# Two more weight splits on VectorE and the memory-weight scaling on ScalarE, in a two-layer decoder on one core

## What is computed

```python
z  = rmsnorm(h) @ w_in                        # columns for four token mixers
h += concat(gla(z_A), pool(z_B), topk_attention(z_C), gated_mlp(z_D)) @ w_out
q  = rmsnorm(h) @ xa_wq                       # cross-attention to 256 memory tokens
kv = rmsnorm(mem, norm_mem) @ xa_wkv
h += attention(q, kv) @ xa_wo
h += swiglu(rmsnorm(h)) if layer == 0 else top2_of_8_experts(rmsnorm(h))
```

## Time and profile before

| | before |
|---|---|
| median of 3 runs (lowest to highest) | 1339.2 us (1338.14 to 1340.39) |
| the profiled execution: its own time | 1333.67 us |
| its span, first to last instruction | 1331.8 us |
| PE busy | 1242.2 us (93%) |
| DVE busy | 545.1 us (41%) |
| ACT busy | 408.4 us (31%) |
| POOL busy | 117.6 us (9%) |
| HBM read | 433.94 MB, 327 GB/s over the span |
| mean granted TensorE clock | 0.986 |

### The profile page before, as it was taken

One profiled execution on the slowest core, in us unless ns is written; L12 is line 12 of the kernel. 1 busy time (PEld: TensorE's weight loads), 2 busy tenths in 40 slices (PEclk: granted clock), 3 DMA queues, 4 the chain that ended last, 5 costly groups with the idle time before them and its releaser, 6 DMA issues.

```text
span 1331.8 us, 15902 instructions
## 1 busy us (share of the span) xinstructions
PE 1242.2 (93%) x6320; PEld 764.5 (57%) x6320; DVE 545.1 (41%) x900; ACT 408.4 (31%) x621; POOL 117.6 (9%) x82
## 2 busy tenths in 40 slices
PE   8999999999999899999989889889889999999876
PEld 6878888888889787334334224224226888434222
DVE  2986387777677936201001001001006999101002
ACT  2852454444364423101001001001005887101002
POOL 0592000000027400000000000000000000000000
PEclk9998999999999999999999999999999999999999
DMA  9733515444425178899999999999999999899996
GB/s 345 306 135 114 218 53 232 169 163 157 197 89 190 63 303 344 357 429 435 430 427 434 431 430 434 426 435 428 432 432 426 428 426 428 371 428 427 427 429 261
DMA packets 32652, 435.84 MB, mean 327 GB/s; under 512 B 5260, under 2 KB 7376, under 8 KB 9296
## 3 DMA queue, kind: packets, MB, share of 16 engines
q1 hardware_dynamic: 32400, 434.48, 78.6%
q0 software_dynamic: 192, 0.53, 0.1%
HBM read 433.94 MB, written 1.05 MB: 327 GB/s over the span
## 4 chain that ended last, share of the span: by engine, by line
PE 60%; DMA 28%; DVE 8%; ACT 2%; SPq 1%; issue 1%; POOL 0%; DVEq 0%
DMA ring<-in_experts 26%; PE bank L2437 14%; PE bank L2530 8%; PE bank L2445 7%; PE bank L2314 6%; PE bank L1887 4%; PE bank L2318 3%; PE bank L1993 3%; PE bank L1861 2%; DMA ring<-in_packed 2%; PE bank L2199 1%; PE bank L2206 1%; PE bank L2200 1%; PE bank L2364 1%; PE bank L2389 1%; DVE score L1306 1%
## 5 line engine op out<-in xcount | busy, mean ns | idle before, releaser
L2437 PE MATMUL bank<-ring,xs 128*64 128x512 f32 x1568 | 362.1, 606 | 38.3 <-DMA ring<-in_experts 38.1
L2437 PEld LDWEIGHTS bank<-ring,xs 128*64 128x64 f32 x1568 | 112.1, 138 | 249.6 <-issue 217.9
L1731 DVE TENSOR_TENSOR s_act<-wsT,bank 128x256 f32<-128x256 f32 x49 | 20.6, 421 | 503.4 <-ACT wsT L1086 503.4
L2445 PE MATMUL bank<-ring,s_act 128*64 128x512 f32 x736 | 173.3, 611 | 23.8 <-DMA ring<-in_experts 23.7
L2445 PEld LDWEIGHTS bank<-ring,s_act 128*64 128x64 f32 x736 | 54.1, 140 | 129.5 <-issue 117.1
L1086 ACT ACTIVATE wsT<-bank 128x256 f32<-128x256 f32 x49 | 18.8, 384 | 331.1 <-PE bank L2389 331.1
L2314 PE MATMUL bank<-x_both,wf_hi 128*128 128x512 f32 x336 | 118.9, 396 | 0.0
L1755 DVE TENSOR_TENSOR w_lo<-ring,w_hi 128x1024 fp32r<-128x1024 f32 x84 | 101.5, 1223 | 12.5 <-ACT w_hi L1144 7.5
L1020 ACT ACTIVATE wf_hi<-ring 128x1024 fp32r<-128x1024 f32 x66 | 69.7, 1060 | 96.9 <-PE bank L2314 66.1
L1144 ACT ACTIVATE w_hi<-ring 128x1024 fp32r<-128x1024 f32 x84 | 89.0, 1061 | 26.5 <-PE bank L2530 23.7
L2318 PE MATMUL bank<-x_both,wf_lo 128*128 128x256 f32 x336 | 94.2, 280 | 0.0
(11 more groups left out here) (392 smaller groups left out, 1685.3 us busy)
## 6 DMA issues: line engine op xcount, KB each, us to landing
ring<-in_experts SPq DMA_DIRECT2D x93, 2048.0 KB, 21.2
ring<-in_experts SPq DMA_DIRECT2D x36, 4096.0 KB, 25.9
ring<-in_packed SPq DMA_DIRECT2D x18, 1536.0 KB, 6.6
ring<-in_packed SPq DMA_DIRECT2D x11, 2048.0 KB, 9.3
ring<-in_packed SPq DMA_DIRECT2D x18, 1024.0 KB, 6.9
extra<-in_experts SPq DMA_DIRECT2D x3, 2048.0 KB, 10.6
ring<-in_packed SPq DMA_DIRECT2D x2, 656.0 KB, 7.3
ring<-in_packed SPq DMA_DIRECT2D x1, 1312.0 KB, 5.5
```

The source lines that it names most:

```text
L2437: i = mm(ps[d % 2][SMALL * side:SMALL * side + SMALL, :], xs[:, k, :], weights(u)[:, at:at + FC], start=k == 0, stop=k == KT - 1)
L2445: i = mm(ps[6 + half][SMALL * side:SMALL * side + SMALL, :], s_act[:, d % 4, x + side, :], weights(UNIT_OF["out", d, 0])[:, at:at + FC], s ...
```

## The change

In both layers POOL no longer scales `xa_wkv` and no longer makes `lo` of row blocks 2 and 3. ACT scales `xa_wkv` in two halves of four instructions each: the first right before its wait for `qe_ready`, the second right before its `hi` of row block 0. DVE makes `lo` of all four row blocks, 2 and 3 first, directly behind the decay masks. The counts of the semaphores follow (`wkv0` and `wkv1` stand in `HI_ORDER`), and PE waits for `wkv1` where it waited for POOL.

```diff
-        HI_ORDER = [(..., "uv0", "uv1", "row2", "row3", "row0", "row1", "row4"),
+        HI_ORDER = [(..., "uv0", "uv1", "wkv0", "row2", "row3", "wkv1", "row0", "row1", "row4"),
...
-        LO_POOL = [("ag", "cv", "wkv", "row2", "row3"), ("cq0", "cq1", "wkv", "row2", "row3")]
+        LO_POOL = [("ag", "cv"), ("cq0", "cq1")]
...
 # gpsimd
-                gp.wait_ge(arrived[U_WKV], landed1)
-                take_wait()
-                for k in range(KT):
-                    w = ring[:, U_WKV, 512 * k:512 * k + 512]
-                    i = gp.tensor_scalar(w, w, pcol[layer][:, R_MEM + k:R_MEM + k + 1], None, ALU.mult)
-                i.then_inc(S["lo_done"], 1)
...
-                for n in (2, 3):
-                    rows_split(n)
...
 # scalar
+                def memory_scaled(part):
+
+                    act.wait_ge(arrived[U_WKV], (layer * (16 * LAYER_TURNS) + 32))
+                    for k in range(KT // 2 * part, KT // 2 * part + KT // 2):
+                        w = ring[:, U_WKV, 512 * k:512 * k + 512]
+                        i = act.activation(w, w, ACT.Copy, scale=pcol[layer][:, R_MEM + k:R_MEM + k + 1])
+                    i.then_inc(S["hi_done"], 1)
+                memory_scaled(0)
                 act.wait_ge(S["qe_ready"], L1)
...
                 act.activation(kdr, v3(ps[2], 0, 256, 2), ACT.Copy).then_inc(S["kdr_done"], 1)
+                memory_scaled(1)
                 rows_split(0)
                 rows_split(1)
...
 # vector
                 i.then_inc(S["att_done"], 1)
-                rows_split(0)
-                rows_split(1)
+                for n in (2, 3, 0, 1):
+                    rows_split(n)
...
 # tensor
-                pe.wait_ge(*lo_from(layer, "wkv"))
+                hi_ready("wkv1")
...
-                    if n in (2, 3):
-                        pe.wait_ge(*lo_from(layer, f"row{n}"))
```

More of the change, by code:

```diff
@@ L536, in row_lo @@
             return ring_lo[ROWS[n]][:, 0:2048]
-        HI_ORDER = [("ag", "x1", "x0", "cv", "bu", "cq0", "cq1", "uv0", "uv1", "row2", "row3", "row0", "row1", "row4"),
-                    ("ag", "cv", "bu", "cq0", "cq1", "x1", "x0", "uv0", "uv1", "row2", "row3", "row0", "row1", "row4")]
-        LO_POOL = [("ag", "cv", "wkv", "row2", "row3"), ("cq0", "cq1", "wkv", "row2", "row3")]
+        HI_ORDER = [("ag", "x1", "x0", "cv", "bu", "cq0", "cq1", "uv0", "uv1", "wkv0", "row2", "row3", "wkv1", "row0", "row1", "row4"),
+                    ("ag", "cv", "bu", "cq0", "cq1", "x1", "x0", "uv0", "uv1", "wkv0", "row2", "row3", "wkv1", "row0", "row1", "row4")]
+        LO_POOL = [("ag", "cv"), ("cq0", "cq1")]
         LO_DVE = [("x1", "x0", "bu", "cq0", "cq1", "uv0", "uv1"), ("ag", "cv", "bu", "x1", "x0", "uv0", "uv1")]
@@ L751, in _ @@
                 first, second = (layer * 2 + 1), (layer * 2 + 2)
-                landed1 = (layer * (16 * LAYER_TURNS) + 32)
                 restart()
```

## The result

| | before | after |
|---|---|---|
| median of 5 runs (lowest to highest) | 1338.14 us (1334.19 to 1340.39) | 1327.29 us (1325.63 to 1330.22) |
| the profiled execution: own time, span, mean granted clock | 1333.67, 1331.8, 0.986 | 1330.22, 1328.4, 0.982 |
| first output product, layer 0 | 115.86 | 114.78 |
| from there to the first output product of layer 1 | 345.12 | 341.02 |

The account below looks back on a forecast made before the run. PE held 60% of the chain and DMA 28%, with the edited stage running through DVE's splits and POOL delaying DVE. Layer 1 -3.7 and layer 0 -0.6 gave -4.3: 1339.2 to 1334.9 us, range 1330.5 to 1339.3.

Parts of the forecast that it names:

- rival (b): Layer 1's gain shrinks to -1.5, layer 0 pays the clock in full (+1.4): 1337.7 to 1339.2 us; chance 0.20.
- Layer 1, forecast -3.7: DVE's split of block 1 ends 2.6 us earlier, and about four fewer POOL collisions save 1.2; ends -4.2 and -1.5.
- PE has no other work on that path which is later: Layer 1: PE's waits there were for DVE, so DVE's saving was counted in full, sum -3.8 us.
- Layer 0, forecast -0.6: First output product 2.5 us earlier through fewer collisions, less 1.9 for a new low clock; ends -6.6 and +1.4.
- Masks: Layer 0: POOL's `memT` multiplies move onto DVE's scan and masks and hold them, +3.1 us (ends 1 and 4.4).
- Copy of `q`: Layer 0: DVE's copy of `q`, which ended at 75.46, would end near 80.3.
- Idle time: Layer 0: PE stands idle about 4.2 us before L1982, waiting for the late copy of `q`.
- The new low clock: Layer 0: PE may run at 0.50 after the new idle stretch; between 0 and 3.8 us, middle 1.9 taken.
- The old one: Layer 0: existing low clock over 100.40 to 108.00, costing at most 3.8 us inside the 115.86, would go.
- ACT, forecast at no cost: Eight added ACT copies of 0.55 us, 2.2 us per half, fit into ACT's waits of 2.45 and 4.58 us.
- the last of the sum: The -4.3 us from the profiled execution, 5.5 us under the median, was applied unchanged to the median: 1334.9 us.
- Rival (a): POOL gets in less often; layer 0 gives -4.6 to -6.6, total 1330.9 to 1328.9 us; chance 0.22.

Follow-up runs that it names:

- no_memT: Changed kernel with one 128x1 instruction instead of POOL's four `memT` multiplies in layer 0; 1371.02 us, not comparable because other experts were chosen.
- after_filled: Changed kernel with 7 unread products (3.2 us) on PE in layer 0 before its wait for the copy of `q`; 1326.26 us, ratio 0.9908 to before.
- l1_only: Changed kernel with layer 0 as in the kernel before, so the change is in layer 1 alone; 1334.33 us, ratio 0.9970 to before.
- filled twin: Kernel changed in layer 1 alone, plus 6 and 4 unread products in PE's two idle times of layer 0; 1331.34 us, ratio 0.9965 to before.
- before_filled2: Kernel before with unread products in PE's idle times, 6 and 4 in layer 0, 4 and 3 in layer 1; 1334.24 us, ratio 0.9968.
- hybrid: Changed kernel with POOL scaling the memory weights in layer 0 as before, ACT in layer 1; 1329.28 us, ratio 0.9941 to before.

## Why the prediction was wrong

**The mechanism held.** POOL's instructions and DVE's exclude each other, and taking POOL's work out of the stage frees DVE. no_memT gives 0.97 us per multiply, most of the 1.25 that one takes undisturbed beside the top-k rounds. The Trainium skill (SBUF — State Buffer, Who interferes with whom) calls the port pair that the two engines share an exclusive lock; the trace agrees. The prediction read this of instructions with two SBUF inputs; a mask with one tensor input was held as well. The Trainium skill's warning about such offloading (Perfetto Trace Analysis, Optimizing Scalar/DVE Operations), my rival (b), did not decide here.

**Layer 1, forecast -3.7, measured -4.1** (345.12 to 341.02). DVE's split of block 1 ends at 435.83, which is 436.9 on before's count (layer 0 is 1.08 earlier) against 436.6 forecast. What I did not see ("PE has no other work on that path which is later") is that PE becomes the bound: its chain runs without a break, so all idle time goes, the 2.00 us before the state products and the 1.89 before L2170 in before's layer 1.

**Layer 0, forecast -0.6, measured -1.1** between the profiled executions. Masks: +3.1 forecast, +3.4 measured (5.69 less 2.26). Copy of `q`: 80.3 forecast, 79.77. Idle time: 4.2 forecast, 3.42. The new low clock: 1.9 taken between 0 and 3.8, and 2.6 measured by after_filled. The old one, which I thought to be inside the 115.86, cost nothing in that place: l1_only, whose layer 0 is that of before, has 115.26 with it, and its filled twin 115.28 without. So the way from the state products to the output products, 15.4 us in before and forecast at 11.8, was not long because of the clock. It came to 11.1 in after (103.67 to 114.78) mainly because DVE was held there: L1415, L1417 and L1418 took 1.12, 0.89 and 0.83 us in before beside POOL's mixer chain (98.80 to 109.70), and 0.41 to 0.43 in after, where that chain ends at 93.73. The size of that term was nearly right, its reason was not.

**ACT, forecast at no cost.** 0.64 us each and not 0.55, and still 3.10 us of waiting before the queries.

**The step that failed** is the last of the sum: "nothing says the stage differs between them, so I carry the microseconds: 1339.2 - 4.3 = 1334.9". The stage does differ. Before's profiled execution, 5.5 us under the median, has its low clock where DVE was late anyway; in the other one that was traced it falls later, and in layer 1 too, and the stage ends 6.5 us later. The change takes away the idle times that come before it, in layer 1 altogether and in layer 0 late in the stage. So it removes a cost that the execution I read did not have, and I gave the median only the part that this execution showed. The account: filling the idle times of before is worth 4.3 to 5.3 us (before_filled2), and from there to the changed kernel it is 5.4 more (1334.24 to 1328.87, across two sets, the fillings' own delay included); for this the first output products show 2.0 in layer 0 and 3.8 in layer 1. The second part is what the forecast summed (4.3); the first was missing. The forecast also carried a gain of the stage to the end in full. The first expert did start 5.2 us earlier, but between the two profiled executions 1.8 us of it were gone at the end, and why is open. Rival (a) named a time nearest to the result, 1328.9 to 1330.9, for a reason that was not so: POOL got in as often as I thought.

What stays open: why the low clock behind the same idle time starts at once in one execution and 9 us later in another, and how often which happens; no run here controls it. How before's executions divide between the two rests on two traces of it, on the times and mean clocks of the others, and on the fillings.

## What to carry to other kernels

When the profiled execution stands well off the median, do not carry its microseconds over: profile the kernel a second time, and look for idle times of PE in the stage that is edited, since the clock may fall behind them in other executions, and put that cost into the forecast with a chance. Filling such an idle time with useless products of known length is a cheap experiment that separates the clock from the wait. And when work is moved off a shared port, ask which engine is late next: here PE took over as the bound, and two quite different halves of the change each gave nearly the whole gain.

## What was not expected of the hardware

- The low clock can come long after the idle time. State products started behind 3.0 to 3.1 us of idle time in three traces: the clock read 0.50 over 100.4 to 108.0 in one, full over 100.3 to 109.3 and then 0.50 over 109.3 to 123.0 in the second, and 0.65, 0.50 and 0.59 over 100 to 107, 107 to 116 and 116 to 124 in the third.
- The low clock also came without such an idle time: 13.7 us of it in hybrid, where PE's longest idle time in the stage was 2.13 us.
- 6.1 us at 0.52 cost 2.6 us on dense products, and 6.6 us at 0.50 cost nothing where DVE was late (115.26 against 115.28).
- POOL's multiplies of 128x512 took 1.25 us each beside DVE's top-k rounds, and 1.7 to 1.9 each beside its masks. A copy of 128x512 with a column scale took ACT 0.64 us.
- A POOL instruction of 64x256 that takes 0.73 us alone took 2.67 us beside DVE's splits of 2.7 us (425.51), while each split lost only 0.45 us (2.73 against 2.28).
